# A new order of the mixer's steps on ScalarE and VectorE, value chunks of 512 rows by 512 columns, and three output chunks begun together

## The chip, the cores and the metric

The kernel runs on one core of a Trainium2 chip. The metric is the device time of one execution in microseconds (us). The kernel before took 2060.58 us, the median of three runs (2059.67 to 2061.08).

## The reference, cut to what matters

The model is a trunk of two layers on 256 tokens of width 1024, all in float32. Each layer has a token mixer, a cross-attention into 256 memory tokens and a feed-forward part (dense in the first layer, two of eight experts in the second). The change touches the mixer and the joints around it:

```
proj = xn @ w_in + b_in            # 512 a, 512 b, 512 pool, 4 x 1024 (q,k,v,z), 8 gates, 3 x 1024 merge gates
u    = silu(layer_norm(causal_conv31(c_a * sigmoid(c_b))));      y_a = u @ w_conv_out
y_b  = pool_mixer(p_u) @ w_pool_out
q, k = silu(causal_conv4([m_q, m_k]));   h = mlstm(q, k, m_v, gates)          # 4 heads of 256
h    = h * rsqrt(mean(h*h)) * g * sigmoid(m_z);                  y_c = h @ w_mlstm_out
y    = g0 * y_a + g1 * y_b + g2 * y_c;   x = x + y @ w_out
x    = x + cross_attention(rms_norm(x), mem)                     # xk, xv from mem; xq; xo
x    = x + swiglu or moe(rms_norm(x))
```

## The kernel before, in words

**Chunks.** Every weight matrix is read in chunks of one megabyte, 128 partitions by 2048 elements. SP loads a chunk into one of three `raw` buffers. ScalarE (ACT) copies it, rounded, into one of three `w_hi` buffers (line 685). VectorE (DVE) writes the rest, `raw - w_hi`, into one of three `w_lo` buffers (line 1079). TensorE (PE) then forms each product as three matmuls, high by high, high by low and low by high (`three`, lines 1656 to 1658). ACT may overwrite `w_hi` of chunk c only when PE has finished chunk c-3.

**The mixer's 63 chunks** stand in the list `MIX`: 0 to 3 `cb`/`ca` (the convolution's input), then `q0 v0 k0 v1 q1 v2 k1 v3` as 4 to 11, `q2 z0 k2 pu0 q3 pu1 k3 z1 z2 z3` as 12 to 21, `gb0 gb1 pw gb2 gb3` as 22 to 26, `wp0 wp1 gc0 gc1 gc2 gc3` as 27 to 32, `wm0..3` as 33 to 36, `ga0..3` as 37 to 40, `wc0 wc1` as 41 and 42, `wo0..3` as 43 to 46, `xk0..3` as 47 to 50, then `xv0`, `xq0..3`, `xv1..3`, `xo0..3`. A chunk of `w_in` is all 1024 input rows by 256 columns. Its products go to one of the PSUM banks 0 to 3, in turn; `pw`, `wp` and `wc` take two banks. `take_banks` makes PE wait until the last content of the bank has been read (`read_by` says by whom).

**What ACT and DVE do.** Both run a loop over c (`mixer`), and in step c they call `post(c-3)`, which is all the work that follows chunk c-3, and then `split(c)`, which makes `w_hi(c)` or `w_lo(c)`; DVE then adds some taps of the 31-tap convolution (`conv31`, line 1146). Each engine does this strictly in that order. The parts of `post` that matter here:

- chunk 4: `forget_rows` on ACT (three small activations with two table loads between them) after two adds on DVE;
- after each q and k chunk: the 4-tap convolution `conv4` on DVE (lines 1130, 1132), `qk_silu` on ACT one step later;
- chunk 5: `gate_scans` on DVE; each v chunk: the bias add into `vx` on DVE (line 1276);
- chunks 11, 15, 19, 23 (`SCORES`): the decay on ACT and GpSimd and `decayed_scores` on DVE; two steps later `hidden` on DVE;
- chunk 26: the root of the hidden state's mean square on ACT; chunk 27: DVE's reciprocal of it (line 1310), then eight copies on ACT that scale `q_t` (line 840). PE transposes `q_t` after the chunk `HIDDEN_T = AT["gc", 0]` (line 1789), which is chunk 29;
- `wp`, `wm`, `wc`: the gated merge into `xf` on DVE; for `wc` also ACT's `merged_hi` (line 772) and DVE's `merged_lo` for each quarter, which are `a_hi`, `a_lo` of the `wo` product.

PE's `project_two` computes the first halves of wo0 and wo1 (which need the quarters 0 and 1 of the merged stream) and then their second halves.

Of the kernel before, what the change touches and what calls it, by code (L numbers as in the profile page):

```python
# [54 lines left out]
MIX += [("gb", 0), ("gb", 1), ("pw", 0), ("gb", 2), ("gb", 3)] + [("wp", i) for i in range(2)]  # L55
MIX += [("gc", i) for i in range(4)] + [("wm", i) for i in range(4)]
# [44 lines left out]
def bank_plan():  # L101


    steps = []
    for c, (kind, i) in enumerate(MIX):
        steps.append((("chunk", c), 2 if kind in ("pw", "wp", "wc") else 1))
    plan, last, n = {}, [None] * 4, 0
    for key, count in steps:
        plan[key] = []
        for part in range(count):  # L110
            plan[key].append((n % 4, last[n % 4]))
            last[n % 4] = (key, part)
            n += 1
    return plan
# [70 lines left out]
def trunk(nc, w, out):  # L185
    ctx = ExitStack()
    with ctx:
# [251 lines left out]
        def chunk_source(layer, c):  # L439
# [7 lines left out]
            first = {"cb": C_B, "ca": C_A, "q": C_Q, "k": C_K, "v": C_V, "pu": C_POOL, "z": C_Z, "ga": C_G, "gb": C_G + D, "gc": C_G + 2 * D}  # L447
# [201 lines left out]
        def read_by(key, part):  # L649
# [13 lines left out]
            return {"cb": b_sig, "ca": u_done, "v": v_done, "pu": pool_pre, "z": z_done, "pw": pw_done, "wo": h_mix, "xk": xk_done,  # L663
# [13 lines left out]
        def _(act):  # L677
# [116 lines left out]
            def post(layer, j):  # L794

# [66 lines left out]
                if kind == "wc":  # L862
                    for q in (2 * i, 2 * i + 1):
                        merged_hi(layer, q)
# [9 lines left out]
                if XQ0 + 1 <= j < XQ0 + 1 + HEADS:  # L874
                    x_exp(layer, j - XQ0 - 1)
                if XQ0 + 2 <= j < XQ0 + 2 + HEADS:
                    x_copy(layer, j - XQ0 - 2)
                for hd in X_OUT_AFTER.get(j, ()):
                    x_out_hi(layer, hd)
                if XO0 <= j < N_MIX:  # L880
                    if layer and j == XO0:
                        act.activation(warm, eps[:, 0:1], ACT.Sqrt)
                    act.wait_ge(h_att.sem, h_att.at(layer, j - XO0 + 1))
                    if layer == 0:
                        for n in (2 * (j - XO0), 2 * (j - XO0) + 1):
                            ins = act.activation(b_hi[:, n, :], h[:, n, :], ACT.Copy, scale=col(0, R_NORM + 16 + n))
                        ins.then_inc(n_hi.sem, 1)
                    square(layer, 2, j - XO0)
                    if layer:
                        for k in (2 * (j - XO0), 2 * (j - XO0) + 1):  # L890
                            ins = act.activation(xf[:, k, :], h[:, k, :], ACT.Copy, scale=col(0, R_NORM + 16 + k))
                        ins.then_inc(xg_done, 1)
# [45 lines left out]
            def mixer(layer):  # L938
# [135 lines left out]
        def _(dve):  # L1074
# [181 lines left out]
            def post(layer, j):  # L1256
                if j == GATE_ROWS:

                    dve.wait_ge(if_mul.sem, if_mul.at(layer, 1))
                    dve.wait_ge(ifb_in.sem, ifb_in.at(layer, 32))  # L1260
                    ch.did(dve.tensor_scalar(rows[:, 0, :], ps[5][0:HEADS, 0:T], if_bias[0:HEADS, :], None, ALU.add))
                    dve.tensor_scalar(rows[:, 1, :], ps[5][32:32 + HEADS, 0:T], if_bias[32:32 + HEADS, :], None, ALU.add).then_inc(if_dve.sem, 1)
                kind, i = MIX[j]
                if j in QK_NO:
                    conv4(layer, QK_NO[j])
                if j == GATE_ROWS + 1:
                    gate_scans(layer)
# [14 lines left out]
                if kind == "ca":  # L1282
# [14 lines left out]
                if j == PW:  # L1297
                    multiplied(layer, j)
                    for g in range(NG):
                        ins = dve.tensor_scalar(pooled[:, g, :], bank(("chunk", j), g // 2)[:, (g % 2) * HALF:(g % 2 + 1) * HALF], col(0, R_PS + g), None, ALU.mult)  # L1300
                    ins.then_inc(pw_done.sem, 1)
# [9 lines left out]
                if kind == "wp":  # L1311
                    merge(layer, j, 2 * i, 2)
# [26 lines left out]
                if kind == "wm":  # L1339
                    merge(layer, j, 4 + i, 1)  # L1340
                if kind == "wc":
                    merge_conv(layer, j, i)
                if WO0 <= j < XK0:
                    residual(layer, j, j - WO0, h_mix)
                if j == WO0:
                    for k in range(KB):
                        dve.wait_ge(mem_hi.sem, mem_hi.at(layer, k + 1))
                        dve.scalar_tensor_tensor(b_lo[:, k, :], mem_t[:, k, :], col(2, R_MEMG + k), as_f32(b_hi[:, k, :]), ALU.mult, ALU.subtract).then_inc(mem_lo.sem, 1)
                if j == XK0 + 1:
                    factor(layer, 1)  # L1350
                    norm(layer, 1, R_NORM + 8, a_hi, a_lo)
                if kind == "xv":
                    x_value(layer, j, i)
                if kind == "xq":
                    multiplied(layer, j)
                    dve.tensor_copy(flat(q_t[:, 2 * i:2 * i + 2, :]), bank(("chunk", j))[:, :]).then_inc(xq_done.sem, 1)
                if XQ0 + 1 <= j < XQ0 + 1 + HEADS:
                    x_probs(layer, j - XQ0 - 1)
                for hd in X_OUT_AFTER.get(j, ()):
                    x_out(layer, hd)  # L1360
                if layer and j == XO0:
                    multiplied(layer, j)
                    ch.did(dve.tensor_scalar(sel_t, h[:, 0, :], 0.0, None, ALU.mult))
                    ch.did(dve.tensor_scalar(y_hi_e, flat2(h)[:, 0:D], 0.0, None, ALU.mult))
# [791 lines left out]
```

## Time and profile before

| | |
|---|---|
| median of three runs | 2060.58 us |
| the profiled execution | 2059.43 us, its span 2057.7 us |
| PE busy | 2025.9 us (98%) |
| DVE busy | 1631.0 us (79%) |
| ACT busy | 1304.1 us (63%) |
| mean granted TensorE clock | 0.996 |

The first layer's mixer ends its wait-rich part at about 340 us, the second layer's mixer begins near 620 us and repeats the first some 605 us later, and the experts run from about 1047 us. A matmul's end is modelled, so that matmuls that follow each other overlap in the list; the distance of two starts is what one costs.

### The profile page before, as it was taken

How to read it: one execution, taken by the hardware profiler on the slowest of the kernel's cores; microseconds unless marked ns; L12 is line 12 of the kernel's file. 1: busy time of each engine (PE TensorE's matmuls, PEld its weight loads, DVE VectorE, ACT ScalarE, POOL GpSimd, SP SyncE). 2: the span in 40 equal slices, each digit the busy share in tenths (PEclk: the TensorE clock that was granted, in tenths of full speed). 3: DMA queues.
4: the chain of work that ended last, by engine and by line, in shares of the span. 5: the costliest groups of instructions: out<-in, count | busy, mean ns of one | idle time of the engine just before them, and what ended most of it. 6: DMA issues, size and time to landing. Idle time of an engine off the chain costs nothing.

```text
span 2057.7 us, 33552 instructions
## 1 busy us (share of the span) xinstructions
PE 2025.9 (98%) x12937; PEld 1843.8 (90%) x12937; DVE 1631.0 (79%) x1652; ACT 1304.1 (63%) x1168; POOL 9.3 (0%) x65
## 2 busy tenths in 40 slices
PE   8999999999999999999999999999999999999997
PEld 8999999999999999999988888888888888888886
DVE  6988866555558988866578898888889888898887
ACT  6666454444346566554467777777777777777776
POOL 0000000000000000000000000000000000000000
PEclk9999999999999999999999999999999999999999
DMA  8545545455554545555469999898999989999995
GB/s 251 174 129 165 185 161 187 138 161 189 184 184 142 183 132 164 170 190 164 161 242 375 335 368 372 321 381 325 367 363 345 375 325 370 342 365 375 321 379 188
DMA packets 309916, 527.23 MB, mean 256 GB/s; under 512 B 13598, under 2 KB 156598, under 8 KB 309814
## 3 DMA queue, kind: packets, MB, share of 16 engines
q1 hardware_dynamic: 309814, 525.81, 73.0%
q8 instruction: 72, 1.18, 0.2%
q14 instruction: 30, 0.25, 0.0%
HBM read 524.73 MB, written 1.05 MB: 256 GB/s over the span
## 4 chain that ended last, share of the span: by engine, by line
PE 80%; DVE 9%; ACT 5%; issue 4%; SPq 1%; DMA 0%; DVEq 0%; ACTq 0%
PE ps L1656 25%; PE ps L1658 24%; PE ps L1657 24%; DVE w_lo L1079 3%; ACT w_hi L685 2%; DVE c L1146 1%; PE ps L2027 1%; ACT w_hi L692 1%; PE ps L2102 1%; PE ps L1806 1%; PE ps L1826 1%; DVE a_lo L1079 1%; PE ps L1721 1%; DVE xf L1103 0%; PE ps L1770 0%
## 5 line engine op out<-in xcount | busy, mean ns | idle before, releaser
L1079 DVE TENSOR_TENSOR w_lo<-raw,w_hi 128x2048 fp32r<-128x2048 f32 (+1 forms) x330 | 752.5, 2282 | 246.9 <-ACT w_hi L685 181.9
L1656 PE MATMUL ps<-w_hi,a_hi 128*128 128x512 f32 (+1 forms) x1472 | 566.2, 385 | 2.2 <-DVE w_lo L1079 2.2
L1658 PE MATMUL ps<-w_hi,a_lo 128*128 128x512 f32 (+1 forms) x1472 | 560.5, 381 | 0.0
L1657 PE MATMUL ps<-w_lo,a_hi 128*128 128x512 f32 (+1 forms) x1472 | 559.6, 380 | 0.0
L1656 PE MATMUL ps<-a_hi,w_hi 128*128 128x256 f32 x1456 | 417.4, 287 | 4.0 <-DVE xf L1197 1.9
L1657 PE MATMUL ps<-a_lo,w_hi 128*128 128x256 f32 x1456 | 412.0, 283 | 0.0
L1658 PE MATMUL ps<-a_hi,w_lo 128*128 128x256 f32 x1456 | 411.8, 283 | 0.0
L692 ACT ACTIVATE w_hi<-raw 128x2048 fp32r<-128x2048 f32 x171 | 328.1, 1919 | 122.4 <-PE ps L1658 122.4
L685 ACT ACTIVATE w_hi<-raw 128x2048 fp32r<-128x2048 f32 (+1 forms) x159 | 299.9, 1891 | 59.0 <-PE ps L1658 42.7
L1658 PEld LDWEIGHTS ps<-w_hi,a_lo 128*128 128x128 f32 x1472 | 276.6, 188 | 53.6
L1656 PEld LDWEIGHTS ps<-w_hi,a_hi 128*128 128x128 f32 x1472 | 276.9, 188 | 53.0 <-DVE w_lo L1079 2.8
L1657 PEld LDWEIGHTS ps<-w_lo,a_hi 128*128 128x128 f32 x1472 | 277.0, 188 | 50.7
L1656 PEld LDWEIGHTS ps<-a_hi,w_hi 128*128 128x128 f32 x1456 | 279.2, 192 | 5.7 <-issue 2.2
L1657 PEld LDWEIGHTS ps<-a_lo,w_hi 128*128 128x128 f32 x1456 | 279.3, 192 | 0.5
L1658 PEld LDWEIGHTS ps<-a_hi,w_lo 128*128 128x128 f32 x1456 | 279.1, 192 | 0.0
L1656 PE MATMUL ps<-b_hi,w_hi 128*128 128x256 f32 x808 | 231.5, 286 | 2.5 <-DVE w_lo L1079 1.4
L1657 PE MATMUL ps<-b_lo,w_hi 128*128 128x256 f32 x808 | 228.6, 283 | 0.0
L1658 PE MATMUL ps<-b_hi,w_lo 128*128 128x256 f32 x808 | 228.6, 283 | 0.0
L1656 PEld LDWEIGHTS ps<-b_hi,w_hi 128*128 128x128 f32 x808 | 155.0, 192 | 4.0 <-DVE w_lo L1079 1.8
L1657 PEld LDWEIGHTS ps<-b_lo,w_hi 128*128 128x128 f32 x808 | 155.0, 192 | 0.3
L1658 PEld LDWEIGHTS ps<-b_hi,w_lo 128*128 128x128 f32 x808 | 155.0, 192 | 0.0
L1079 DVE TENSOR_TENSOR w_lo<-mem_t,w_hi 128x2048 fp32r<-128x2048 f32 x56 | 128.4, 2292 | 21.6 <-ACT w_hi L692 21.6
(314 smaller groups left out, 2144.6 us busy)
## 6 DMA issues: line engine op xcount, KB each, us to landing
raw<-in_moe_w SPq DMA_DIRECT2D x171, 1024.0 KB, 6.0
raw<-in_w_in SPq DMA_DIRECT2D x68, 1024.0 KB, 5.2
mem_t<-in_moe_w SPq DMA_DIRECT2D x56, 1024.0 KB, 5.7
area<-in_moe_w SPq DMA_DIRECT2D x56, 1024.0 KB, 5.7
xf<-in_moe_w SPq DMA_DIRECT2D x56, 1024.0 KB, 5.3
raw<-in_ffn_w SPq DMA_DIRECT2D x33, 1024.0 KB, 5.3
raw<-in_w_mlstm_out SPq DMA_DIRECT2D x8, 1024.0 KB, 5.0
raw<-in_w_out SPq DMA_DIRECT2D x8, 1024.0 KB, 5.0
```

The lines of the kernel that those rows point to most:

```text
L685: act.activation(w_hi[c % SPL][:, 0:n], raw[c % RAW][:, 0:n], ACT.Copy).then_inc(hi_done.sem, 1)
L692: act.activation(w_hi[m % SPL][:, :], e_raw[m % ERAW][:, 0:CH], ACT.Copy).then_inc(e_hi.sem, 1)
L1079: return dve.tensor_tensor(dst, whole, as_f32(hi), ALU.subtract)
L1146: ins = dve.scalar_tensor_tensor(dst, src, tap, dst, ALU.mult, ALU.add)
L1656: pe.matmul(dst, wh, xh, start=start, stop=False, skip_group_check=True)
L1657: pe.matmul(dst, wh, xl, start=False, stop=False, skip_group_check=True)
L1658: return pe.matmul(dst, wl, xh, start=False, stop=stop, skip_group_check=True)
L1721: ins = pe.matmul(ps[4][:, 0:T], ones[:, :], sq[:, j % 2, i * T:(i + 1) * T], start=(j == 0 and i == 0), stop=(j == 3 and i == 1), skip_gr ...
L1806: ins = pe.matmul(ps[4 + hd % 2][:, tt * T:(tt + 1) * T], q_t[:, k, tt * P:(tt + 1) * P], k_t[:, k, :], start=(tt == 0 and e == 0), stop=( ...
L1826: ins = pe.matmul(ps[X_OUT_BANK[hd]][:, e * T:(e + 1) * T], vx[:, m, hd, e * P:(e + 1) * P], z_sig[:, 4 + 2 * (hd % 2) + m, :], start=(e = ...
L2027: ins = pe.transpose(ps[6][:, k * P:(k + 1) * P], act_e[g % 2][:, k * P:(k + 1) * P], ident[:, :])
L2102: ins = pe.matmul(ps[7 - i][:, k * P:(k + 1) * P], h_tok[:, tt, c:c + P], sel[:, tt, :], start=(k == 0 and tt == 0), stop=(tt == 1), skip_ ...
```

## The change

The list `MIX` puts `gc0` between `wp0` and `wp1`, so that `gc0` is chunk 28, `wp1` chunk 29. The line `HIDDEN_T = AT["gc", 0]` is as before and now means 28. Value chunks are 512 input rows by 512 columns; v0 and v1 are the two row halves of the same columns and are accumulated in the same two banks, and so are v2 and v3.

`post` becomes `first` and `later`, and in step c both engines do `first(c-3)`, `split(c)`, `later(c-3)`. In `first` are the operations that read a chunk's bank, the merges and the whole of the cross-attention; in `later` are, on DVE, the adds for the gate rows, `conv4`, `gate_scans`, the copy of the gate columns, `pooling`, the low parts of the pooled values, `decayed_scores`, `hidden`, the reciprocal for the hidden state, both layer-norm steps, the gating and low parts of the hidden state, the memory's low parts and the norm ahead of the cross-attention; on ACT their counterparts. `project_two` becomes `project_three`.

```diff
-MIX += [("gb", 0), ("gb", 1), ("pw", 0), ("gb", 2), ("gb", 3)] + [("wp", i) for i in range(2)]
-MIX += [("gc", i) for i in range(4)] + [("wm", i) for i in range(4)]
+MIX += [("gb", 0), ("gb", 1), ("pw", 0), ("gb", 2), ("gb", 3), ("wp", 0), ("gc", 0), ("wp", 1)]
+MIX += [("gc", i) for i in range(1, 4)] + [("wm", i) for i in range(4)]
...
-        steps.append((("chunk", c), 2 if kind in ("pw", "wp", "wc") else 1))
+        count = 2 - 2 * (i % 2) if kind == "v" else 2 if kind in ("pw", "wp", "wc") else 1
+        steps.append((("chunk", c), count))
...
+            if kind == "v":
+                rows, c0 = slice((i % 2) * 512, (i % 2 + 1) * 512), C_V + (i // 2) * 512
+                return at_layer(w["w_in"], layer)[:, rows, c0:c0 + 512].rearrange("o (k p) n -> p (o k) n", p=P)
...
+            if kind == "v":
+                return v_done, i + part + 1
...
                 for c in range(SPL + layer, N_MIX + SPL):
-                    post(layer, c - SPL)
+                    first(layer, c - SPL)
                     if c < N_MIX:
                         split(layer, c, chunk_len(c))
+                    later(layer, c - SPL)
...
-                if kind == "v":
-                    hd = i
+                if kind == "v" and i % 2:
                     multiplied(layer, j)
                     dve.wait_ge(vb_in.sem, vb_in.at(layer, 16))
+                    c0 = (i - 1) * DH
                     for tt in range(TT):
-                        ins = dve.tensor_tensor(vx[:, tt, hd, 0:DH], bank(("chunk", j))[:, tt * DH:(tt + 1) * DH], vb_pool[:, hd * DH:(hd + 1) * DH], ALU.add)
-                    ins.then_inc(v_done.sem, 1)
+                        dve.tensor_tensor(vx[:, tt, i - 1:i + 1, 0:DH], bank(("chunk", AT["v", i - 1]), tt)[:, :].rearrange("p (e d) -> p e d", e=2),
+                                          vb_pool[:, c0:c0 + 2 * DH].rearrange("p (e d) -> p e d", e=2), ALU.add).then_inc(v_done.sem, 1)
...
-            def project_two(layer, c, xh, xl, ready):
+            def project_three(layer, c, xh, xl, ready):
                 for part in range(2):
-                    for j in (c, c + 1):
+                    for j in (c, c + 1, c + 2):
                         if part == 0:
                             pe.wait_ge(lo_done.sem, lo_done.at(layer, j + 1))
                             take_banks(layer, ("chunk", j))
...
+            def project_pair(layer, c, i, xh, xl):
+                pe.wait_ge(lo_done.sem, lo_done.at(layer, c + 1))
+                first = AT["v", i - i % 2]
+                if i % 2 == 0:
+                    take_banks(layer, ("chunk", c))
+                wh, wl = weights(c, 4)
+                for k in range(4):
+                    x = 4 * (i % 2) + k
+                    for tt in range(TT):
+                        t = slice(tt * P, (tt + 1) * P)
+                        ins = three(bank(("chunk", first), tt)[:, :], xh[:, x, t], xl[:, x, t], wh[:, k, :], wl[:, k, :], x == 0, x == KB - 1)
+                ins.then_inc(pe_chunk.sem, 1)
...
-                pe.wait_ge(v_done.sem, v_done.at(layer, hd + 1))
+                pe.wait_ge(v_done.sem, v_done.at(layer, 2 * (hd // 2) + 2))
```

In the second layer the three DVE operations that clear tiles for the experts move from ahead of chunk 59's residual to behind `split(62)`.

## Rows read from the trace of the kernel before

**Rows 1.** The page: the span, and busy time, share and instructions by engine.
```profile
span 2057.7 us, 33552 instructions
PE 2025.9 (98%) x12937; PEld 1843.8 (90%) x12937; DVE 1631.0 (79%) x1652; ACT 1304.1 (63%) x1168; POOL 9.3 (0%) x65
```
**Rows 2.** The waits of PE: total us, times, longest.
```profile
PE ps L1656 <- DVE w_lo L1079: 6.3, 9, 1.3
```
**Rows 3.** PE's timeline, matmuls after a stall: start, us, [idle before <- releaser].
```profile
72.59 0.39 PE L1656 MATMUL ps<-w_hi,a_hi 128*128 128x256 f32 x1 [0.72 <-DVE w_lo L1079]
...
192.90 0.36 PE L1656 MATMUL ps<-b_hi,w_hi 128*128 128x256 f32 x1 [0.53 <-issue]
...
199.82 0.35 PE L1656 MATMUL ps<-a_hi,w_hi 128*128 128x256 f32 x1 [0.94 <-DVE xf L1197]
...
225.54 0.39 PE L1656 MATMUL ps<-b_hi,w_hi 128*128 128x256 f32 x1 [0.72 <-DVE w_lo L1079]
...
263.95 0.39 PE L1656 MATMUL ps<-a_hi,w_hi 128*128 128x256 f32 x1 [0.18 <-DVE w_lo L1079]
...
295.35 0.39 PE L1656 MATMUL ps<-a_hi,w_hi 128*128 128x256 f32 x1 [0.91 <-DVE a_lo L1079]
...
339.09 0.39 PE L1656 MATMUL ps<-w_hi,b_hi 128*128 128x256 f32 x1 [1.18 <-DVE w_lo L1079]
...
677.58 0.38 PE L1656 MATMUL ps<-w_hi,a_hi 128*128 128x256 f32 x1 [1.31 <-DVE w_lo L1079]
```
**Rows 4.** PE's timeline: second and 48th matmul of v2; two of an expert.
```profile
72.81 0.28 PE L1657 MATMUL ps<-w_lo,a_hi 128*128 128x256 f32 x1
...
78.33 0.28 PE L1658 MATMUL ps<-w_hi,a_lo 128*128 128x256 f32 x1
...
1304.22 0.39 PE L1656 MATMUL ps<-w_hi,a_hi 128*128 128x512 f32 x1
...
1308.07 0.40 PE L1658 MATMUL ps<-w_hi,a_lo 128*128 128x512 f32 x1
```
**Rows 5.** ACT's and DVE's timelines, steps 7 to 9.
```profile
51.44 0.42 ACT L734 ACTIVATE z_sig<-z_sig 4x256 f32<-4x256 f32 x1 [4.47 <-DVE z_sig L1262]
...
55.23 1.90 ACT L685 ACTIVATE w_hi<-raw 128x2048 fp32r<-128x2048 f32 x1
...
57.16 2.29 DVE L1079 TENSOR_TENSOR w_lo<-raw,w_hi 128x2048 fp32r<-128x2048 f32 x1 [2.60 <-ACT w_hi L685]
...
72.44 0.76 DVE L1276 TENSOR_TENSOR vx<-ps,vb_pool 128x256 f32<-128x256 f32 x2
```
**Rows 6.** Busy time by stretch: length, PE, PEld, DVE, ACT, POOL, clock, DMA.
```profile
57.16:72.54 15.38, 14.71 (x123) 14.50 (x121) 15.21 (x25) 11.39 (x11) 0.00 (x0) 1.00 0.45 137
174.81:198.93 24.12, 23.51 (x188) 22.80 (x186) 21.46 (x38) 11.92 (x15) 0.00 (x0) 1.00 0.54 173
...
1035.80:1038.80 3.00, 3.00 (x16) 3.00 (x16) 2.66 (x21) 2.80 (x6) 0.00 (x0) 0.50 0.00 0
...
2046.50:2049.20 2.70, 0.00 (x0) 0.00 (x0) 0.73 (x3) 1.76 (x7) 0.00 (x0) 1.00 0.02 6
2049.50:2052.50 3.00, 0.00 (x0) 0.00 (x0) 2.02 (x4) 0.00 (x0) 0.00 (x0) 0.51 0.56 196
```
**Rows 7.** Timelines around the hidden state: PE behind chunk 23, DVE, ACT.
```profile
169.92 0.69 PE L1765 MATMUL ps<-m_row,selh 4*128 4x256 f32 x2
...
198.93 0.20 DVE L1310 RECIPROCAL small<-small 128x8 f32<-128x8 f32 x1
...
199.16 3.31 ACT L840 ACTIVATE q_t<-q_t,small 128x256 f32<-128x256 f32 x8 [4.06 <-DVE small L1310]
```
**Rows 8.** Timelines around `wc` and `wo`: ACT, PE, DVE.
```profile
275.83 0.84 ACT L714 ACTIVATE area<-ps,par 128x256 f32<-128x256 f32 x2 [3.12 <-PE ps L1658]
...
287.08 0.28 PE L1656 MATMUL ps<-a_hi,w_hi 128*128 128x256 f32 x1
...
296.41 2.29 DVE L1079 TENSOR_TENSOR w_lo<-raw,w_hi 128x2048 fp32r<-128x2048 f32 x1 [1.11 <-ACT w_hi L685]
```

More of the change, by code:

```diff
@@ L792, in x_out_hi, with first @@
                 act.activation(flat(a_hi[:, 2 * hd:2 * hd + 2, :]), ps[X_OUT_BANK[hd]][:, :], ACT.Copy).then_inc(xo_hi.sem, 1)
-            def post(layer, j):
+            def first(layer, j):
                 kind, i = MIX[j]
@@ L873, in post @@
                     norm_hi(layer, 1, a_hi)
[L874 to L892, printed above, removed]
             def ahead(layer, m):
@@ L1291, in post, with later @@
                     ins.then_inc(u_done.sem, 1)
+                if j == PW:
+                    multiplied(layer, j)
+                    for g in range(NG):
+                        ins = dve.tensor_scalar(pooled[:, g, :], bank(("chunk", j), g // 2)[:, (g % 2) * HALF:(g % 2 + 1) * HALF], col(0, R_PS + g), None, ALU.mult)
+                    ins.then_inc(pw_done.sem, 1)
+                if kind == "wp":
+                    merge(layer, j, 2 * i, 2)
+                if kind == "wm":
+                    merge(layer, j, 4 + i, 1)
+                if kind == "wc":
+                    merge_conv(layer, j, i)
+                if WO0 <= j < XK0:
+                    residual(layer, j, j - WO0, h_mix)
+                if kind == "xv":
+                    x_value(layer, j, i)
+                if kind == "xq":
+                    multiplied(layer, j)
+                    dve.tensor_copy(flat(q_t[:, 2 * i:2 * i + 2, :]), bank(("chunk", j))[:, :]).then_inc(xq_done.sem, 1)
+                if XQ0 + 1 <= j < XQ0 + 1 + HEADS:
+                    x_probs(layer, j - XQ0 - 1)
+                for hd in X_OUT_AFTER.get(j, ()):
+                    x_out(layer, hd)
+                if XO0 <= j < N_MIX:
+                    residual(layer, j, j - XO0, h_att)
+                    if layer == 0 and j > XO0:
+                        gained_lo(j - XO0 - 1)
+            def later(layer, j):
+                kind, i = MIX[j]
+                if j == GATE_ROWS:
+                    dve.wait_ge(if_mul.sem, if_mul.at(layer, 1))
+                    dve.wait_ge(ifb_in.sem, ifb_in.at(layer, 32))
+                    ch.did(dve.tensor_scalar(rows[:, 0, :], ps[5][0:HEADS, 0:T], if_bias[0:HEADS, :], None, ALU.add))
+                    dve.tensor_scalar(rows[:, 1, :], ps[5][32:32 + HEADS, 0:T], if_bias[32:32 + HEADS, :], None, ALU.add).then_inc(if_dve.sem, 1)
+                if j in QK_NO:
+                    conv4(layer, QK_NO[j])
+                if j == GATE_ROWS + 1:
+                    gate_scans(layer)
+                if j == GATE_ROWS + 6:
+                    dve.wait_ge(if_tr.sem, if_tr.at(layer, 1))
+                    dve.tensor_copy(gcols[:, :], ps[6][:, 0:16]).then_inc(gcols_done.sem, 1)
                 if j == AT["pu", 1]:
@@ L1297, in post @@
                 if j == PW:
[L1298 to L1301, printed above, removed]
                     dve.wait_ge(pw_hi.sem, pw_hi.at(layer, 1))
@@ L1348, in post @@
                         dve.scalar_tensor_tensor(b_lo[:, k, :], mem_t[:, k, :], col(2, R_MEMG + k), as_f32(b_hi[:, k, :]), ALU.mult, ALU.subtract).then_inc(mem_lo.sem, 1)
+                if layer and j == XO0:
+                    ch.did(dve.tensor_scalar(sel_t, h[:, 0, :], 0.0, None, ALU.mult))
+                    ch.did(dve.tensor_scalar(y_hi_e, flat2(h)[:, 0:D], 0.0, None, ALU.mult))
+                    ch.link(dve.tensor_scalar(y_lo_e, flat2(h)[:, 0:D], 0.0, None, ALU.mult))
                 if j == XK0 + 1:
@@ L1351, in post @@
                     norm(layer, 1, R_NORM + 8, a_hi, a_lo)
[L1352 to L1364, printed above, removed]
-                    ch.link(dve.tensor_scalar(y_lo_e, flat2(h)[:, 0:D], 0.0, None, ALU.mult))
-                if XO0 <= j < N_MIX:
-                    residual(layer, j, j - XO0, h_att)
-                    if layer == 0 and j > XO0:
-                        gained_lo(j - XO0 - 1)
                 if layer and j == XK0:
@@ L1832, in chunk @@
                 if kind == "v":
-                    project_tokens(layer, c, a_hi, a_lo)
+                    project_pair(layer, c, i, a_hi, a_lo)
                 elif kind == "pw":
@@ L1861, in chunk @@
                     if i == 0:
-                        project_two(layer, c, a_hi, a_lo, y_lo)
-                    elif i > 1:
+                        project_three(layer, c, a_hi, a_lo, y_lo)
+                    elif i > 2:
                         project(layer, c, a_hi, a_lo)
```

62 lines of the change are left out of this document (33 added, 29 removed).

## The prediction

> **What bounds the kernel now.** I read the page first, then PE's waits, then PE's timeline, looking at the distance from one matmul's start to the next, and last the timelines of DVE and ACT wherever that distance opens. The page shows PE busy in 98% of the span and no other engine above 80% [rows 1]. So the reader should see that time can be won in two ways only: less work on PE, or fewer of its stalls; whatever makes PE stall anew is lost one for one. The waits show how little the stalls hold: the largest kind, PE waiting for `w_lo`, comes to 6.3 us in nine times [rows 2]. The timeline places them [rows 3]. A matmul of 256 columns is drawn 0.28 us long but the next starts 0.12 us after it, so a stall costs the idle time in the row plus 0.16 us. The first layer's mixer then has seven: 0.88 us ahead of v2, 0.69 ahead of wp1, 1.10 ahead of gc0 (its bank waits for the merge), 0.88 ahead of wm0, 0.34 ahead of ga2, 1.07 inside wo1 (`a_lo`), 1.34 ahead of xv0. The second layer repeats them 605 us later, with 1.47 us ahead of v2 [rows 3], where 0.32 us had been lost two chunks before. All but the one in wo1 come from an order: the engine that is to deliver does other work first.
>
> **Value chunks, PE's side.** A matmul of 256 columns starts every (78.33 - 72.81) / 46 = 0.120 us, one of 512 columns every (1308.07 - 1304.22) / 17 = 0.2265 us [rows 4]. A value chunk has 48 of the first kind, 5.76 us, and will have 24 of the second, 5.44 us: -0.32 us each, -1.28 us per layer, if PE is what is waited for.
> The Trainium skill, page "TensorE: Matmul & The Clock Gate", section "Wait — 56ns, not 53.3ns?", gives a start-to-start of N / 2.4 GHz plus about 2.5 ns, that is 109 and 216 ns. These rows show 120 and 226.5 ns, so about 13 ns of fixed cost in place of 2.5. By the page a chunk would win 0.06 us and all eight 0.5 us; the rows win 2.6 us, and the rows decide.
>
> **Value chunks, the new wait.** In the bank plan v0 takes banks 1 and 2 and keeps them until v1 is done; v2 takes the same two. They come free when DVE has added the bias, which it now does in `first(7)`, in step 10, behind `later(6)`, that is behind `conv4` of k0. Follow DVE from step 7. The two adds for the gate rows now stand behind `split(7)`, 2.2 us later; `forget_rows` took from 51.44 to 55.23 us [rows 5], so it now ends at 57.4, and `w_hi(8)`, behind it on ACT, at 59.4. From there DVE has what it had from 57.16 to 72.54 us, 15.2 us busy [rows 6], less `split(7)` (2.2) and the add for v0 (0.7), plus the adds of the pair (twice the 0.76 us that two small ones take [rows 5], about 1.4 as larger pieces): 13.7 us. The banks come free at 73.1 us. PE, without a stall, would be there at 71.7 - 0.64 = 71.1. So v2 starts at 73.15 where it started at 72.59 [rows 3]: **+0.56 us** per layer in place of the gain of v0, v1 and the old stall together. v2 and v3 then bring **-0.64**. The second layer's DVE and PE stand to each other there as in the first, 604.99 us later on both. Bounds for the sum of both: -1.5 (banks free in time) to +1.
>
> **wp1 and gc0.** With `pw`'s copies behind `split(27)` and gc0 ahead of wp1 there is a chunk's time for the merge of wp0, so both stalls go: **-0.69 and -1.10**.
>
> **The hidden state, a new wait.** `HIDDEN_T` follows gc0 and is now chunk 28, so PE asks for the scaled `q_t` one chunk (5.8 us) sooner. What delivers it is chained: DVE's reciprocal in `later(27)`, which now stands behind the merge of wp0 and behind `split(30)`; then eight copies on ACT, 3.2 us [rows 7]. DVE's queue from `split(26)`: ACT can make `w_hi(26)` once chunk 23 is multiplied (169.9 us [rows 7], then its gate 0.75 and the copy 1.9), so DVE starts at 172.7, where it started at 174.81 [rows 6]; the decay that stood between now comes behind. Old work from there to the reciprocal is 21.46 us [rows 6]. To it come `decayed_scores` with the wait for GpSimd's mask (1.3), the merge (1.2) and `split(30)` (2.2): 26.2 us, so the reciprocal stands at 198.9, the last copy ends at 202.4, and PE has its transposes done at 202.8. PE had wp0 done at 192.90 - 0.69 = 192.2 [rows 3]; it is 0.08 sooner with the two value terms, and gc0 follows it in 5.8 us, at 197.9; PE would have had the 16 transposes done 1.3 us after. Stall: **+3.7 us** per layer. It is at least 1.0 (DVE never behind, then the merge waits for wp0 and the rest follows) and at most about 5.5 (each exchange between the engines 0.2 us dearer and the decay late). I take 3.7, since the sum is of rows.
>
> **wm0, ga2, xv0.** There `w_lo` now precedes the low parts of the hidden state, the layer norm and the cross-attention norm, and what these deliver is wanted a chunk or more later: **-0.88, -0.34, -1.34**. For the last I checked what is late next: the norm takes until about 12.5 us after xk1, xq0 wants it at 17.8 us.
>
> **`project_three`.** It begins wo2 (chunk 45) right after the first halves of wo0 and wo1, and so wants `w_lo(45)` 5.8 us after it starts at 287.08: at 292.85 us. But DVE makes `w_lo(45)` at 296.41 to 298.70 [rows 8]. This time doesn't depend on PE at that point: it follows from chunk 40's gate at 275.83 [rows 8] by `split(43)`, the merges of wc0 with their exchanges with ACT, `split(44)`, the merges of wc1 and `split(45)`, and merges stand in `first`, ahead of the split, as before. Now PE did the second halves of wo0 and wo1 in this time and lost 1.07 us; then it waits 5.85 us with those halves queued behind the wait: **+5.85 - 1.07 = +4.78 us** per layer. `w_hi(46)` waits for the end of wo0, some 8 us later than now, but comes 1.5 us before PE wants it. Bounds +4.3 and +5.3.
> The clock adds to it. After the last matmul of the run the granted clock was still 1.00 for 2.7 us and then 0.51 [rows 6], so a wait of 5.85 us is long enough to fall from 2.4 to 1.2 GHz; when it fell during the routing it stayed at 0.50 for 3.0 us of busy PE [rows 6]. Half of 3.2 us is **+1.6 us** per layer; bounds 0 and 2.5.
> The Trainium skill, page "TensorE: Matmul & The Clock Gate", section "HAM oscillation — how this bites in real kernels", says that waits between bursts of matmuls send the array back to the lower clock and cost half of the throttled time. The rows of the run's end and of the routing agree with it.
>
> **The sum.** Per layer +0.56 - 0.64 - 0.69 - 1.10 + 3.7 - 0.88 - 0.34 + 4.78 - 1.34 = +4.05, with the clock +5.65; two layers +11.3 us. The profiled execution took 2059.43 us (its span 2057.7 and 1.7 around it): 2070.7. The median of the runs lies 1.15 above it: **2072 us**. Moving the clearing of tiles behind `split(62)` and the value loads (2 KB pieces for 1 KB, while the DMA queues are half idle [rows 6]) I cost at nothing; if the queue were full, a late chunk would show as ACT waiting for DMA.
>
> **Rivals.**
> 1. Only `project_three` bites. For it: DVE's queue ahead of the reciprocal is a sum of 15 parts, and 3.7 us of lateness is a small difference of large numbers. Against it: even an idle DVE leaves 1.0 us. Gain over my sum 7.4 us: 2064.5.
> 2. Only the hidden wait bites, `w_lo(45)` is there in time. For it: nothing in the rows but that the split-first order makes ACT and DVE earlier elsewhere. Against: the merges still come first. 2072 - 2 x (5.85 + 1.6) = 2057.
> 3. The other side, faster: DVE runs ahead. The mechanism is the split-first order at step c, which takes ACT's waits out of DVE's queue (2.7 us of the 24.1 between `split(26)` and the reciprocal were idle [rows 6]); if that gathers from pooling on, both the hidden state and `w_lo(45)` are there when asked for, and all old stalls and the PE saving remain. It decides if DVE reaches the reciprocal before about 195 us and `w_lo(45)` before 293. 2072 - 7.4 - 14.9 = 2049.7.
> 4. The clock falls at the hidden wait too, where the transposes come in four thin groups over 5 us: +1.6 per layer, 2075. If it falls nowhere: 2068.7.
>
> **Chances.** My forecast with rival 4, 2066 to 2078: 0.66. Rival 1: 0.14. Rival 2: 0.07. Rival 3: 0.10. Something slower still: 0.03. About 0.2% (4.1 us) is what a measurement of this kernel can tell from no change. Faster, below 2056.5: rival 3 and a part of rival 2, 0.14. Within: 0.14. Slower, above 2064.7: 0.72. Cases of both signs hold chances, so the range reaches to rival 1 and the near end of rival 2, 2058, and up to all upper bounds, 2079; the forecast's own range is 2066 to 2078.
>
> **What would show it.** A matmul of wo2 (an `a_hi` one) after some 5.7 us of idle time put down to DVE's `w_lo`, once per layer, and a granted clock under 1.00 around it; four groups of transposes (line of `hidden_transpose`) spread over about 5 us after gc0, released by ACT's `q_t`; v2 starting behind DVE's `vx` with some 1.9 us of idle; no stall ahead of wp1, wm0, ga2, xv0; 512-column matmuls of the value chunks 0.2265 us apart. I am wrong if PE has no idle time of over 3 us in the wo chunks, or if the transposes follow gc0 without a gap.

## The result and the profile after

The changed kernel took **2075.53 us**, the median of four runs (2075.39 to 2075.73), against 2060.24 us for the kernel before in the same comparison (2059.67 to 2061.08): a ratio of 1.0072, 95% interval 1.0058 to 1.0085. The change makes it slower by 15 us. The forecast was 2072, with a range of 2058 to 2079. The profiled execution took 2075.39 us, 15.96 more than that of before.

The page of the changed kernel, against [rows 1]: the span is 15.9 us longer, with 192 matmuls fewer.

```profile
span 2073.6 us, 33156 instructions
...
PE 2031.6 (98%) x12745; PEld 1840.9 (89%) x12745; DVE 1630.5 (79%) x1644; ACT 1304.6 (63%) x1168; POOL 10.3 (0%) x65
```

The waits of PE in the changed kernel (total us, times, longest). Nine small waits for `w_lo` [rows 2] have become two of 5.7 us, and three kinds are new: `vx` is v2's banks, `q_t` the hidden state. The third, `a_lo` L1418, is one wait at 15.29 us, in the first layer's norm. It does not come from the change: two of the kernels below, e6_only_order and e8_order_mix, have the same code up to there, and one waits 1.91 us and the other not at all.

```profile
PE ps L1670 <- DVE w_lo L1088: 11.5, 2, 5.7
...
PE ps L1670 <- DVE vx L1272: 3.3, 2, 2.9
PE ps L1817 <- ACT q_t L869: 3.0, 2, 1.5
PE ps L1670 <- DVE a_lo L1418: 2.0, 1, 2.0
```

PE's timeline of the changed kernel, the matmuls behind a stall, against [rows 3]: v2, the transposes and what follows them, and wo2's first matmul, in the first layer and in the second. Nothing over 0.3 us stands any more ahead of wp1, gc0, wm0, ga2 or xv0.

```profile
73.52 0.47 PE L1670 MATMUL ps<-w_hi,a_hi 128*128 128x512 f32 x1 [0.38 <-DVE vx L1272]
...
200.19 3.57 PE L1817 MATMUL ps<-ident,q_t 128*128 128x128 f32 x16 [1.51 <-ACT q_t L869]
...
299.68 0.58 PE L1670 MATMUL ps<-a_hi,w_hi 128*128 128x256 f32 x1 [5.74 <-DVE w_lo L1088]
...
684.49 0.47 PE L1670 MATMUL ps<-w_hi,a_hi 128*128 128x512 f32 x1 [2.92 <-DVE vx L1272]
...
812.78 3.05 PE L1817 MATMUL ps<-ident,q_t 128*128 128x128 f32 x16 [1.53 <-ACT q_t L869]
...
911.39 0.58 PE L1670 MATMUL ps<-a_hi,w_hi 128*128 128x256 f32 x1 [5.73 <-DVE w_lo L1088]
```

DVE's and ACT's timelines of the changed kernel, against [rows 5, 7]. The adds of a pair of value chunks take 1.29 us together; the reciprocal stands at 199.00, where the prediction had 198.9.

```profile
72.08 1.29 DVE L1272 TENSOR_TENSOR vx<-ps,vb_pool 128x512 f32<-128x512 f32 x2
...
199.00 0.19 DVE L1344 RECIPROCAL small<-small 128x8 f32<-128x8 f32 x1
```

```profile
199.23 3.30 ACT L869 ACTIVATE q_t<-q_t,small 128x256 f32<-128x256 f32 x8 [4.29 <-DVE small L1344]
```

Four stretches of the changed kernel in which the granted clock (third column from the right) is low with PE at work: the transposes of the first layer, wo2, v2 of the second layer, the routing.

```profile
201.20:203.80 2.60, 2.60 (x14) 2.40 (x14) 0.00 (x0) 2.58 (x5) 0.00 (x0) 0.50 0.93 329
299.68:303.80 4.12, 4.12 (x20) 4.12 (x21) 0.00 (x0) 0.00 (x0) 0.00 (x0) 0.54 0.71 232
685.00:689.00 4.00, 4.00 (x12) 3.18 (x11) 4.00 (x8) 1.22 (x1) 0.00 (x0) 0.60 0.32 71
1047.50:1061.50 14.00, 12.71 (x62) 12.65 (x62) 6.88 (x43) 6.65 (x10) 0.00 (x0) 0.51 0.51 183
```

The kernel before had a low clock in two parts of its routing, with full speed between:

```profile
1035.30:1038.80 3.50, 3.50 (x20) 3.50 (x20) 3.12 (x25) 2.80 (x6) 0.00 (x0) 0.57 0.00 0
1039.20:1042.00 2.80, 1.51 (x15) 1.45 (x13) 1.43 (x9) 2.80 (x4) 0.00 (x0) 1.00 0.38 90
1042.40:1045.80 3.40, 3.40 (x19) 3.40 (x19) 1.30 (x7) 0.60 (x1) 0.00 (x0) 0.53 1.07 410
```

**Stage lengths.** Whole runs scatter by some us, and the traces show the clock low for longer in some executions than in others. Distances between fixed matmuls of the mixer scatter by a few hundredths of a us where the clock is 1.00. The start of the kernel does not: up to the fourth head's scores the kernel before and e5_only_three, whose code is the same there, are 0.42 us apart. So I cut each trace at these places of PE's timeline (here the changed kernel's first layer: the fourth head's scores, the layer norm's first sums, the first sum of squares in wo, the cross-attention's first scores):

```profile
170.27 0.69 PE L1793 MATMUL ps<-m_row,selh 4*128 4x256 f32 x2
...
238.52 1.67 PE L1823 MATMUL ps<-c,ones 128*128 128x256 f32 x7
...
313.15 1.13 PE L1749 MATMUL ps<-cacc,ones 128*128 128x256 f32 x4
...
362.75 1.89 PE L1834 MATMUL ps<-k_t,q_t 128*128 128x256 f32 x8
```

V is from the first sum of squares at the second layer's entry to its first scores, A from the fourth scores to the layer-norm sums, B on to wo's sum of squares, C on to the cross-attention's scores, R from the router's first matmul to the first transposes inside the experts (`ps<-ident,vx`). Two numbers are first / second layer, in us; a star marks a stage with the clock at 0.50 for a part of PE's work in it (B has it behind the wait, R always in part, and fully where starred).

| kernel | V | A | B | C | R |
|---|---|---|---|---|---|
| before | 77.91 | 67.23 / 67.21 | 68.38 / 68.36 | 50.94 / 50.93 | 42.61 |
| changed | 79.59* | 68.25* / 67.38 | 74.63* / 74.31* | 49.60 / 49.60 | 45.21* |
| e1_two | 77.99 | 68.48* / 68.38* | 67.96 / 67.94 | 49.49 / 49.49 | 45.17* |
| e2_hidden | 79.56* | 64.57 / 64.56 | 74.74* / 75.62* | 49.60 / 49.60 | 43.85 |
| e3_bank | 74.96 | 67.37 / 67.38 | 74.80* / 74.93* | 49.60 / 49.60 | 42.63 |
| e9_filler | 79.44* | 68.45* / 68.47* | 72.97 / 72.97 | 49.61 / 49.61 | 43.61 |
| e5_only_three | 77.91 | 67.24 / 67.22 | 75.60* / 75.09* | 50.94 / 50.93 | 42.30 |
| e6_only_order | 75.96 | 64.54 / 64.55 | 67.93 / 67.93 | 49.49 / 49.49 | 42.61 |
| e7_only_v | 79.55* | 67.21 / 67.21 | 68.36 / 68.36 | 50.93 / 50.93 | 42.64 |
| e4b_all_two | 74.96 | 64.53 / 64.53 | 67.93 / 67.94 | 49.49 / 49.49 | 45.19* |
| e8_order_mix | 75.95 | 67.37 / 67.37 | 67.95 / 67.93 | 49.50 / 49.49 | 42.33 |
| e10_order_pair | 74.94 | 64.56 / 64.56 | 67.92 / 67.92 | 49.50 / 49.50 | 45.19* |
| e12_three_early | 74.94 | 64.55 / 64.55 | 67.59 / 67.57 | 49.59 / 49.60 | 43.79 |

Changed less before: up to the first layer's fourth scores +0.35, A +1.02 and +0.17, B +6.25 and +5.95, C -1.34 and -1.33, V +1.68, R +2.60, which makes 15.35 of the 15.9 us. The +0.35 is within the scatter of the start.

### The profile page after: what moved, and what is told of

Same layout as the page of the kernel before. It is cut to its first block, busy times and chain, and to the rows that moved or that the text cites. A ratio compares the mean times of both kernels' runs of the same rounds, so it can differ in the third digit from the quotient of the medians.

```text
span 2073.6 us, 33156 instructions
## 1 busy us (share of the span) xinstructions
PE 2031.6 (98%) x12745; PEld 1840.9 (89%) x12745; DVE 1630.5 (79%) x1644; ACT 1304.6 (63%) x1168; POOL 10.3 (0%) x65
## 3 DMA queue, kind: packets, MB, share of 16 engines
q8 instruction: 70, 1.15, 0.2%
HBM read 524.73 MB, written 1.05 MB: 254 GB/s over the span
## 4 chain that ended last, share of the span: by engine, by line
PE 85%; DVE 7%; ACT 4%; issue 3%; DMA 1%; DVEq 0%; SPq 0%; POOL 0%; ACTq 0%
PE ps L1670 26%; PE ps L1672 26%; PE ps L1671 26%; DVE w_lo L1088 3%; ACT w_hi L691 2%; DVE c L1155 1%; PE ps L2055 1%; ACT w_hi L698 1%; DMA raw<-in_w_in 1%; PE ps L2130 1%; PE ps L1834 1%; PE ps L1854 1%; PE ps L1749 1%; PE ps L1798 0%; PE ps L2119 0%
## 5 line engine op out<-in xcount | busy, mean ns | idle before, releaser
L1670 PE MATMUL ps<-w_hi,a_hi 128*128 128x512 f32 x1408 | 555.6, 395 | 3.3 <-DVE vx L1272 3.3
L1672 PE MATMUL ps<-w_hi,a_lo 128*128 128x512 f32 x1408 | 549.9, 391 | 0.0
L1671 PE MATMUL ps<-w_lo,a_hi 128*128 128x512 f32 x1408 | 548.9, 390 | 0.0
L1670 PEld LDWEIGHTS ps<-w_hi,a_hi 128*128 128x128 f32 x1408 | 264.9, 188 | 56.3 <-issue 3.7
L1672 PEld LDWEIGHTS ps<-w_hi,a_lo 128*128 128x128 f32 x1408 | 264.6, 188 | 56.4
L1671 PEld LDWEIGHTS ps<-w_lo,a_hi 128*128 128x128 f32 x1408 | 265.1, 188 | 53.1
```

The costliest lines, as they stand in the source:

```text
L1670: pe.matmul(dst, wh, xh, start=start, stop=False, skip_group_check=True)
L1671: pe.matmul(dst, wh, xl, start=False, stop=False, skip_group_check=True)
L1672: return pe.matmul(dst, wl, xh, start=False, stop=stop, skip_group_check=True)
```

## The experiments

Kernels of one comparison ran on one chip; the medians of before in the three were 2061.15, 2060.71 and 2061.0 us. The first four start from the changed kernel.

**e1_two**: project_two again.

```diff
-                    for j in (c, c + 1, c + 2):
+                    for j in (c, c + 1):
...
-                    elif i > 2:
+                    elif i > 1:
```

> The changed kernel with project_two in place of project_three: wo2 is asked for only after both halves of wo0 and wo1. My theory: the wait of 5.7 us for w_lo(45) (trace of the changed kernel) is mostly work displaced, so per layer 5.85 - 1.07 = 4.8 us come back, and some 2 us more because the granted clock is 0.50 from 296 to 303.8 us around that wait. 2 x 6.8: 2075.5 - 13.6 = about 2062, no wait ahead of wo2 over 0.5 us, clock 1.00 there. Rival a, the low clock costs nothing since it falls in the idle time: 2075.5 - 9.6 = 2066. Rival b, later stages catch up, since DVE and not PE sets the pace from wo to xk: 2073 to 2075.5.

Measured: 2060.36 us (2058.11 to 2062.47), ratio to before 0.9995 (0.9986 to 1.0004). B falls by 6.67 and 6.37 us. In its place stands the old stall:

```profile
298.17 0.38 PE L1670 MATMUL ps<-a_hi,w_hi 128*128 128x256 f32 x1 [0.91 <-DVE a_lo L1088]
```

So one function carries nearly all of the loss, and nothing later catches up: rival b of the expectation falls. In this trace v2 of the second layer waited 2.93 us too, but the clock stayed at 1.00 behind it: V is 77.99, not 79.6. In the first layer it waited 1.98 us, and there the clock did fall, from 73.5 to 77.0 us.

**e9_filler**: 48 matmuls are added whose result nobody reads.

```diff
                         if part == 0:
+                            if j == c + 2:
+                                wh, _ = weights(c, KB)
+                                for n in range(48):
+                                    pe.matmul(ps[6][:, 0:T], wh[:, 0, 0:P], xh[:, 0, :], start=True, stop=True)
                             pe.wait_ge(lo_done.sem, lo_done.at(layer, j + 1))
```

> The changed kernel with added work: ahead of the wait for w_lo(45), PE does 48 matmuls of 256 columns into a bank that nobody reads, 5.76 us at the pitch of 0.120 us, in place of idling 5.7 us. It prices the clock alone, since the matmul of wo2 can start no sooner. If the low clock behind the wait costs what I think, half of the 3.8 us for which it is low with PE busy behind 299.68, the time falls by about 1.9 us per layer: about 2071.5, with the clock 1.00 throughout wo2. Rival: the clock costs nothing because DVE is what is waited for there as well: 2075.5 or, by the little that the added matmuls overrun, 2076.

Measured: 2072.16 us (2069.25 to 2073.93), ratio 1.0052 (1.0038 to 1.0065). B is 1.66 and 1.34 us shorter with 96 matmuls more. The window around wo2's start, at full clock:

```profile
297.50:302.50 5.00, 5.00 (x42) 4.82 (x41) 2.29 (x1) 0.64 (x1) 0.00 (x0) 1.00 0.12 33
```

The term that I had at 5.85 - 1.07 + 1.6 = 6.38 splits into 72.97 - 67.95 = 5.02 for the wait and 1.3 to 1.7 for the clock. How large the clock's part is follows from the pitch. At 0.50 the changed kernel starts a matmul of 256 columns every (303.26 - 300.06) / 15 = 0.213 us, where it is 0.120 us at 1.00:

```profile
300.06 0.41 PE L1671 MATMUL ps<-a_lo,w_hi 128*128 128x256 f32 x1
...
303.26 0.39 PE L1671 MATMUL ps<-a_lo,w_hi 128*128 128x256 f32 x1
```

So 1 - 0.120 / 0.213 = 44% of the low time is lost. The clock stays low for 3.8 and 3.1 us behind the two waits, which makes 1.66 and 1.35, and B shows 1.66 and 1.34. In the traces of e2_hidden and e3_bank below, which have the same wait, it stays low for 4.0 to 6.0 us, and B is 1.8 to 2.7 us over the 72.97 of this run. The Trainium skill, page "TensorE: Matmul & The Clock Gate", section "HAM oscillation — how this bites in real kernels", puts the loss at half of the throttled time; for the 3.8 us behind 299.68 that is an estimate of 1.9, and this pair of traces shows 1.66.

**e2_hidden**: the transposes a chunk later.

```diff
-HIDDEN_T = AT["gc", 0]
+HIDDEN_T = AT["wp", 1]
```

> The changed kernel with HIDDEN_T moved from chunk 28 (gc0) to chunk 29 (wp1), so that PE asks for the scaled q_t one chunk (5.8 us) later, as before the change. My theory: the stall there, 3.6 us in the first layer and 3.1 in the second, goes, with the low clock from 201.0 to 204.3 us; nothing after it is late: 2075.5 - 6.7 to 8 = 2067.5 to 2069. Rival: DVE and not PE sets the time from there on (the hidden state's low parts are made behind the same queue), so the same time is lost ahead of wm0: 2075.5, with a wait of 3 us there.

Measured: 2066.64 us (2064.91 to 2071.18), ratio 1.0028 (1.0017 to 1.0039). A is 64.57 and 64.56: shorter than in the changed kernel by 3.68 and 2.82, and than in the kernel before by 2.66. The transposes follow without a gap, 1.91 us for all 16:

```profile
204.28 1.91 PE L1817 MATMUL ps<-ident,q_t 128*128 128x128 f32 x16
```

Of the 8.9 us in the median the two stages hold 6.5. Of the rest, R gives 1.36 and B, with a longer low clock in this trace, takes 1.42 back; what makes up the median's remainder is not shown, since the other executions have no trace.

**e3_bank**: `values`, called in `later(j)` ahead of `conv4` for the value chunk j+1, holds the two adds.

```diff
+                if j + 1 < N_MIX:
+                    values(layer, j + 1)
                 if j == GATE_ROWS:
```

> The changed kernel with the two bias adds of a pair of value chunks issued at the head of what DVE does a step later in the order of the step before, ahead of conv4 instead of behind it. My theory: v2 no longer waits for its banks: -0.55 us in the first layer, and in the second -2.9 for the wait of 2.9 us less what v0 and v1 had gained, plus half of the 4.9 us during which the clock is 0.50 behind that wait (2.4). But the hidden state's stall hangs on DVE and not on PE, so what PE gains before it is given back there. Theory: about 1 us less in the first layer before that stall and 3 to 5 in the second, of which at most 1 is left behind the hidden state and the rest becomes a longer wait there, unless DVE itself had waited for PE in between: 2071 to 2075, and the stall ahead of the transposes grows. Rival: all of it stays, 2070.

Measured: 2066.72 us (2065.55 to 2066.94), ratio 1.0026 (1.0015 to 1.0037). V is 4.63 shorter, the wait of 2.92 with its low clock. My theory's second half was wrong, and the rival right: the fourth scores come 2.29 us sooner (167.98), DVE's reciprocal 2.28, and the transposes 2.27, with the same wait ahead of them as in the changed kernel:

```profile
196.72 0.20 DVE L1349 RECIPROCAL small<-small 128x8 f32<-128x8 f32 x1
...
197.92 3.05 PE L1822 MATMUL ps<-ident,q_t 128*128 128x128 f32 x16 [1.53 <-ACT q_t L869]
```

So PE and DVE move together. The other traces bear it out: the reciprocal stands 28.72 to 28.76 us behind the first matmul of the fourth scores in all ten kernels with the new order, and 29.00 to 29.02 in the three with the old one, though the scores themselves come between 167.98 and 171.91 us. DVE's chain to it begins at work that PE delivers. The result lies 3 us below the rival's 2070 as well. That is clock: in this trace it did not fall at the transposes (A -0.88 in the first layer), and R is 2.58 shorter.

The next three take one part of the change into the kernel before.

**e5_only_three**: e1's edit the other way round.

> The kernel before with one part of the change alone: project_three in place of project_two. Theory: w_lo(45) comes at a time that PE doesn't set, so the wait of some 5.8 us arises here too, less the 1.07 us inside wo1, and the low clock behind it costs what the added matmuls showed, 1.3 to 1.7 us: per layer 4.8 + 1.5 = 6.3. 2061 + 12.6 = about 2073.5. Rival: in the kernel before, where split comes last in a step, PE falls behind elsewhere and takes the time up again: 2061 to 2066.

Measured: 2074.08 us (2073.26 to 2075.39), ratio 1.0063 (1.0049 to 1.0077). B +7.22 and +6.73, all other stages within 0.5 us of before. The wait is the same to 0.01 us as in the changed kernel, in which ACT and DVE work in another order:

```profile
299.15 0.58 PE L1656 MATMUL ps<-a_hi,w_hi 128*128 128x256 f32 x1 [5.73 <-DVE w_lo L1079]
```

B grew by more here than in the changed kernel because the clock stayed low for longer behind the waits, 5.5 and 4.3 us; 44% of that is 2.4 and 1.9, which leaves 4.8 for the wait itself, the forecast's 4.78.

**e7_only_v**: the value chunks alone.

```diff
-                if kind == "v":
+                if kind == "v" and i % 2:
...
-                    project_tokens(layer, c, a_hi, a_lo)
+                    project_pair(layer, c, i, a_hi, a_lo)
```

> The kernel before with the third part alone: the value chunks as 512 rows by 512 columns over a pair of banks. Theory: v2 waits for its banks here too, since DVE makes the adds of a pair in the step in which it had made that of v1, behind conv4 of k0: it had them at 72.44, 0.76 us long; now they take 1.4 and end at about 73.2 to 73.9, against v2's start at 72.59 before: +0.6 to +1.3 per layer, less 0.64 for v2 and v3, and perhaps 1.7 per layer for a low clock behind a wait of 2 to 3 us. 2061 to 2065; I take 2062. Rival: the banks are no wait in this order, and PE keeps the 2.6 us of the shorter matmuls: 2058.5.

Measured: 2063.28 us (2059.65 to 2064.31), ratio 1.0007 (0.9998 to 1.0016): no difference that can be told. V is +1.64 with a low clock, and both layers wait for their banks:

```profile
73.55 0.77 PE L1662 MATMUL ps<-w_hi,a_hi 128*128 128x512 f32 x1 [2.13 <-DVE vx L1282]
...
680.11 0.47 PE L1662 MATMUL ps<-w_hi,a_hi 128*128 128x512 f32 x1 [2.23 <-DVE vx L1282]
```

**e6_only_order**: `first`, `split`, `later`, with the tiles for the experts cleared where the changed kernel clears them; MIX, the value chunks and `project_two` as before.

```diff
-                    post(layer, c - SPL)
+                    first(layer, c - SPL)
                     if c < N_MIX:
                         split(layer, c, chunk_len(c))
+                    later(layer, c - SPL)
```

> The kernel before with another part of the change alone: first, split, later in place of post, split on ACT and DVE; MIX, the value chunks and project_two as before. Theory: the stalls for w_lo behind other work go in both layers, v2 0.88 and 1.47 us, wm0 0.88, ga2 0.34, xv0 1.34: -7.5, so 2053.5. Rival a: pw's copies now stand behind a split of 2.2 us, so that wp1 or gc0, which had waited 0.69 and 1.10 us, wait up to 2.2 us more per layer: 2058. Rival b: a stall for w_lo is only given on to the next thing that DVE owes: 2060 to 2061.

Measured: **2047.79 us** (2047.63 to 2048.46), ratio 0.9936 (0.9923 to 0.995), 13 us faster where I had 7.5. Its whole list of PE's waits from 0.2 us on:

```profile
PE ps L2005 <- DMA wdk<-in_norm_mix_g: 5.6, 1, 5.6
PE ps L1667 <- DVE a_lo L1415: 1.9, 1, 1.9
PE ps L1667 <- DVE a_lo L1085: 1.8, 2, 0.9
PE ps L1916 <- DVE xf L1409: 1.4, 1, 1.4
PE ps L2042 <- DVE vx L1513: 1.3, 1, 1.3
PE ps L1667 <- DVE b_lo L1085: 0.4, 2, 0.2
PE ps L1916 <- DVE rstd L1404: 0.4, 1, 0.4
```

Of the mixer's stalls over 0.2 us only the one in wo1 (`a_lo` L1085) is left. A is 2.68 shorter than before, which is the sum of the old stalls ahead of wp1, gc0 and wm0, 0.69 + 1.10 + 0.88 = 2.67 [rows 3]. I had left the first two in this expectation, because I took the new MIX for what removes them; with them it would have been 7.5 + 2 x 1.79 = 11.1. The stages A, B, C and V hold 11.1 of the 11.9 us by which the two traces differ, and the start 0.6.

**e8_order_mix**: e6 with the new MIX.

> The kernel with the new order of first, split and later alone (e6_only_order, 2047.8) plus the new MIX, that is gc0 ahead of wp1 with HIDDEN_T behind gc0; value chunks and project_two as before. Theory: in the new order MIX has nothing left to win, since wp1 and gc0 no longer wait, and asks for the scaled q_t a chunk too soon. From the fourth scores to ln_sums the trace with all but project_three took 68.48 and 68.38 us, the one with the order alone 64.54 and 64.55: +7.8 us, so 2055.6, and up to 2058 if the routing runs at the low clock. Rival: the hidden state's lateness came from the value chunks' wait for banks, which delayed DVE: 2048 to 2049.

Measured: 2055.49 us (2052.47 to 2057.57), ratio 0.9972 (0.9961 to 0.9984). A is 67.37 in both layers, +2.82, with the clock at 1.00; so that is the bare price of asking a chunk too soon, and the value chunks have no part in it. In two layers it is 5.65 us of the 7.7 between the medians of this run and e6; the rest is not placed, since the profiled execution was the fastest of the seven. So my expectation of 7.8 was met in part by luck: it took over e1's A, in which the clock had fallen.

```profile
198.65 3.05 PE L1814 MATMUL ps<-ident,q_t 128*128 128x128 f32 x16 [1.52 <-ACT q_t L866]
```

The three last ones look for a better version.

**e4b_all_two**: the edits of e1, e2 and e3 together in the changed kernel.

> The changed kernel with three repairs together: project_two for wo, HIDDEN_T behind wp1, and the bias adds of the value pairs ahead of conv4. If the three are independent, as the traces of the single repairs suggest (each kept its gain to the end of the layer), their sum counts: 2075.5 - 15.1 - 8.9 - 8.8 = 2042.7, and the ratio to the kernel before is 0.991. Rival: with PE earlier by 4 us at the hidden state in each layer, DVE is what is waited for in gb to wm, and a part comes back as waits for w_lo or b_lo there: 2048 to 2052.

Measured: 2048.16 us (2045.6 to 2049.57), ratio 0.9933 (0.9919 to 0.9946). Stage by stage the repairs do add up: V, A, B and C each have the length of the single repair. The medians don't: their sum gave 2042.7, 5.5 us less than measured. The single runs had, beside their repairs, a shorter low clock than the changed kernel in some stages, worth 1.60 us in V (e1), 1.36 in R (e2) and 2.58 in R (e3), and this trace has R at 45.19; in other stages it went the other way (B of e2, +1.42), so that the account of the medians is not closed. The expectation's rival named the right time, but not the reason: no wait of over 0.2 us stands between gb and wm.

**e10_order_pair**: e6 with the paired value chunks and e3's place for the adds; the old MIX and project_two.

> The new order alone plus the paired value chunks, with their two bias adds ahead of conv4. Theory: the banks are free in time and PE keeps the difference of pitch, 4 x 0.32 us per layer: 2047.8 - 2.6 = 2045.2, if the routing's clock falls for as long as in e6_only_order; if it is 0.50 throughout, as in the trace of the three repairs, 2048. Rival: nothing is won, the wait only shrinks below what the waits table shows: 2047.8.

Measured: **2046.11 us** (2045.38 to 2049.69), ratio 0.9927 (0.9913 to 0.994), the lowest median, though its interval overlaps those of e6, e4b and e12. V is 1.02 shorter than in e6; in the profiled run R is 2.58 longer.

**e12_three_early**: e10 with project_three, and `split(45)` ahead of `first(42)`.

```diff
+                    if c == WO0 + 2:
+                        split(layer, c)
                     first(layer, c - SPL)
-                    if c < N_MIX:
+                    if c < N_MIX and c != WO0 + 2:
```

> e10_order_pair with project_three put back, but with split(45) issued on ACT and DVE ahead of what they do first in that step, that is ahead of the merges of wc1. Theory: w_lo(45) is then made some 3.3 us sooner on DVE (in the changed kernel's trace the four operations between, 290.60 to 295.53 and their waits for ACT, stand ahead of it), so it waits at most for some tenths of a us, and the stall of 1.05 us inside wo1 (a_lo) goes, since PE does wo2's first half meanwhile: -2.1 us, about 2043 to 2046 by the routing's clock. Rival: the merges, 3 us later, make the second halves of wo0 and wo1 wait for a_lo, as much as is won or more: 2045 to 2050.

Measured: 2046.66 us (2046.13 to 2046.88), ratio 0.9931 (0.9917 to 0.9945), the same as e10. The wait for `w_lo(45)` is gone, but B is only 0.33 us shorter, not 1.05: PE still halts in wo, for what the trace does not name, and DVE's merges of wc1 now stand behind two splits in a row (4.49 us).

```profile
288.37 0.36 PE L1679 MATMUL ps<-a_hi,w_hi 128*128 128x256 f32 x1 [0.37 <-issue]
```

```profile
282.45 4.49 DVE L1090 TENSOR_TENSOR w_lo<-raw,w_hi 128x2048 fp32r<-128x2048 f32 x2 [1.11 <-ACT w_hi L691]
286.87 0.68 DVE L1221 TENSOR_TENSOR area<-area,ps 128x512 f32<-128x512 f32 x1
```

## Why the prediction came out as it did

The mechanism and the sign were right, and so was the step that decides: `project_three` had 6.38 us per layer in the sum, and e1 shows 6.67 and 6.37, of which e9 gives 5.02 to the wait (I had 4.78) and 1.3 to 1.7 to the clock (I had 1.6). How long the clock stays low behind that wait was 3.1 to 6.0 us in eight cases of four traces, so a hit to a tenth on this part is luck. The other steps, in their order:

- **v2's banks.** The adds ended at 73.37, for 73.1 in the prediction, and v2 began at 73.52, for 73.15. I summed v0 to v3 to -0.08 per layer. Where the clock stayed up, V shows +0.08 (e1), so the sum was near; the wait in it was 2.93 us, where I had some 1.9. But V of the changed kernel shows +1.68: I let the clock fall only at the long waits, and it fell behind this one of 2.92 us too, for some 1.6 us (79.59 against e1's 77.99). In the first layer the clock had been low from 16.8 to 20.2 us already, which brought PE to v2 some 1.5 us later, and the wait absorbed that: it was 0.38 us, where e1, whose start had full clock, shows 1.98. That the first layer shows no more than +0.35 is therefore luck.
- **wp1 and gc0.** The sum was right (-1.79), its cause wrong. The order removes these stalls by itself (e6), and the new place of gc0 wins nothing on top of it (e8; A is 64.53 in e4b, which has it, and 64.56 in e10, which hasn't).
- **The hidden state.** The reciprocal was placed to 0.1 us, yet the price was 2.82, not 3.7 (e8). Counted from the fourth scores, PE was ready for the transposes after 28.3 us, where I had 28.0; without a wait they would have taken it 1.66 us, where I had 1.3; and it was through with them after 32.74, where I had 32.9. It fell with the clock to 68.25 - 67.37 = 0.9 more in the first layer, which is rival 4 in one layer of two. (With this wait in five traces, the clock fell in both layers of e1 and e9, in one of the changed kernel and in none of e3 and e8.) A, all four of its terms together, had +1.03 in the sum and shows +1.02 and +0.17. My lower bound of 1.0 held; what I added when I wrote e3's expectation, that the lateness hangs on DVE and not on PE, did not.
- **wm0, ga2, xv0.** -0.88 is within e6's A; C fell by 1.34 and 1.33 for my -1.34; B of e6 is 0.45 and 0.43 below before, for -0.34.
- **The 512-column matmuls.** Where nothing waits, V wins 1.02 us per layer (e10 against e6), for my 1.28. By the pitch that the Trainium skill gives, page "TensorE: Matmul & The Clock Gate", section "Wait — 56ns, not 53.3ns?", it would be about 0.25 per layer, an estimate; the measurement is nearer to the rows of this kernel.
- **The 3.5 us between 2072 and 2075.5.** The sum had nothing for R (+2.60, the clock at 0.50 for 13.7 us on end rather than twice 3.4), the layers took 12.75 for my 11.3, and the experts 0.55; against it, the median lay 0.14 above the profiled execution and not 1.15.

Rivals 1 to 3 are refuted by the trace: both waits are there, in both layers. Rival 3, faster by DVE running ahead, gave 2049.7; e6, with the waits left out, shows that the order alone can do that.

**Open.** What decides whether R has the low clock throughout (45.2) or in parts (42.3 to 43.9) is not shown. It changed between executions of one kernel (e10's five runs: four within 2045.38 to 2046.14, and one of 2049.69, which is the profiled one), though the four runs of the changed kernel lay within 0.4 us. So of the 15.3 us, 2.6 are not tied to any part of the change. Nor is it shown what decides whether the clock falls behind a wait of 2 to 3 us, or how long it then stays low.

## What to carry to other kernels

A change of several parts can hold its whole gain in one of them: here the order was worth 13 us, the early hidden state cost 6 to 9 and the third chunk 13 to 15, and the paired chunks gained nothing until the adds that free their banks had moved too. Before work is begun sooner on the engine that bounds the kernel, look up when its input is made, and whether that time moves with the engine (the hidden state, e3) or not (`w_lo(45)`, behind the merges): every microsecond asked too soon is lost, and a wait that stands ahead of ready work (the second halves) costs its full length. Cut the traces at fixed instructions and compare stage lengths; they agree to some hundredths, where whole runs differ by 4 us with the clock.

## What the runs showed of the hardware that I had not expected

The granted clock fell to 0.50 behind waits as short as 2 to 3 us, but not each time. At v2 it fell behind 1.98 us in e1's first layer, 2.13 and 2.23 in e7, and 2.92 in the changed kernel; it did not behind 2.47 in e9's first layer and 2.93 in e1's second. At 15 us, in the first norm, it fell behind 1.87 us in e10 and not behind 1.91 in e6. At transposes in four thin groups it fell in one layer and not in the other (A 68.25, 67.38). Behind the wait of 5.7 us it fell in all eight cases of four traces.

A fall cost 0.9 to 1.1 us at the transposes, 1.5 to 1.6 at v2, 1.3 to 2.7 at wo2. At wo2 the cost was 44% of the time that the clock stayed low with PE at work, in each of the six cases that compare with e9's 72.97 (3.1 to 6.0 us low, 1.34 to 2.65 us lost), as the two pitches have it, 0.213 us and 0.120. Matmuls that do no useful work, in place of the idle time, kept it at 1.00 and won 1.7 and 1.3 us.
